# Value products of the recurrent mixer ahead of the weight group in the odd steps

## The chip, the cores and the metric

The kernel runs on one core of one Trainium2 chip. The metric is the device time of one execution in microseconds (us). Before the change it is 2569.6 us, the median of 3 runs (2569.27 to 2570.37).

## The reference

A sequence of 512 tokens of width 1024 goes through one first block and then two hybrid layers. A hybrid layer normalizes its input, projects it with a wide matrix, and gives the result to four mixers: a recurrent one (A, an mLSTM in both directions), grouped-query attention (B), neighbourhood attention (C) and differential attention (D). Each mixer's output is projected up, gated and added; an output projection and a feed-forward network follow. The change touches mixer A alone:

```
h_fwd = mlstm_scan(qh, kh, vh, i_fwd, jax.nn.log_sigmoid(f_fwd))
flip = lambda t: jnp.flip(t, axis=2)
h_bwd = flip(mlstm_scan(flip(qh), flip(kh), flip(vh), flip(i_bwd), flip(jax.nn.log_sigmoid(f_bwd))))
h = h_fwd + h_bwd
```

with 4 heads of width 128. The kernel computes it without the recurrence, as two masked products: for each head and direction P = (k q) x exp(decay mask), then the numerator P v and the denominator P 1, and the quotient with max(|denominator|, exp(-m)).

## The kernel before, in words

All tokens stand on chip in 4 tiles of 128. Each dense projection is a *block*: its weights come in units of 2 x 128 rows and 512 columns (512 KB), through 3 raw slots and 2 split slots. SyncE's queue loads a unit when the raw slot is free (L527), ScalarE makes its high part wH (L1046), VectorE the low part wL (L1591), and TensorE multiplies high by high, low by high and high by low. The function `group` (L638, L641) does this for one unit and one output tile: 2 row chunks x 3 = 6 matmuls of 512 columns. A group counts `groups` up, which lets ScalarE reuse a split slot.

The mixer is the function `mlstm`, with 36 steps, in each of the two layers; the profile shows them from about 444.6 and 1558.8 us. Its side work is a list of 36 groups (the blocks G00, G01 and the first unit of CQ), one for each step, which keep TensorE supplied while ScalarE and VectorE work on the scan. Steps 0 to 31 go through head h = s // 8, key chunk j = (s % 8) // 2, and direction: an even step is forward, an odd one (back = 1) backward. One step on TensorE, in the old order:

1. the mask product into bank 6 (TP): a row product (L824), 128 to 512 columns wide, and a bf16 causal mask (L826); it waits for the exponential of the step before (e_done);
2. even steps only: the scores k q into bank 4 or 5 (L834), used by this step and the next;
3. the weight group of the side work (L641);
4. the value product (L852), t + 1 chunks forward or 4 - t backward, each chunk two matmuls of 129 columns in the trace, into the one bank 7 (PV).

ScalarE takes the exponential of the mask (L1470). VectorE multiplies it with the scores into pmat (L2385, counts p_done), and drains the value product with four instructions that depend on each other: L2395, L2396, L2398 and L2404 (forward, writes) or L2401 (backward, adds); the last counts hh_done. Then every fourth step (s % 4 == 1) VectorE splits a weight unit (L1591).

Which value product a step carries is written in SCAN_VALUES. An odd step s < 32 has the forward product of its own head and tile. An even step from 8 on has a backward product of the head before. Steps 32 to 35 have the last head's backward products, in banks 7 and 6 in turn. A value product waits for

```python
pe.wait_ge(S["p_done"], i0 + (8 * (h + 1) if back else s))
if s == 1:
    evacuated(by_name[(l + 1, "AV")])
...
if nth >= 1:
    pe.wait_ge(S["hh_done"], nth - 1 if tail else nth)
```

that is, for the multiplications of all steps before it (forward), and for the drain of the value product before it (in the tail: the one before that). In step 1 it also waits until ScalarE has evacuated block AV, the values. The order on VectorE is: multiplication of step s, drain of the product of step s, split. On ScalarE: exponential of step s, then a split (s % 4 == 0) or a gate evacuation (L1145). The multiplication of an odd step stands behind the drain of the even step before it.

Of the kernel before, what the change touches and what calls it, by code (L numbers as in the profile page):

```python
# [271 lines left out]
def scan_step(s):  # L272

    h, j, back = s // 8, s % 8 // 2, s % 2
    lo, hi = (0, (j + 1) * P) if back else (j * P, SEQ)
    return h, j, back, lo, hi
# [23 lines left out]
def build(nc, a, out):  # L300
# [8 lines left out]
    with ctx:  # L309
# [156 lines left out]
        def wsrc(b, k0, kn):  # L466
            name, _, l = b.weight.partition(":")
            w = a[name]
            w = w[int(l) if l else 0]
            return w[b.row0 + k0 * P:b.row0 + (k0 + kn) * P, b.col0:b.col0 + b.cols].rearrange(  # L470
                "(k p) n -> p k n", p=P)
# [5 lines left out]
        def w_views(u):  # L477
            b, k0, kn, _ = units[u]
            width = P if b.gates else b.cols
            return [w[:, u % W_SLOTS, 0:kn * width].rearrange("p (k n) -> p k n", k=kn) for w in (wH, wL)]  # L480
# [65 lines left out]
        def _(pool):  # L546
# [23 lines left out]
            for g, (_, (ki, half)) in list(enumerate(row_groups(fox_items())))[2:]:  # L570
                r = slice(DH * half, DH * half + DH)
                pool.wait_ge(S["hi_done"], g + 1)
                pool.tensor_tensor(k_low[g % 2][r, :], k2[r, ki, :], k_twice[g % 2][r, :].bitcast(F32),
                                   ALU.subtract).then_inc(S["k_low_done"], 1)
# [39 lines left out]
        def _(pe):  # L614
# [3 lines left out]
            def group(b, i, t, chunk=None):  # L618

                u = b.first_unit + i  # L620
                _, k0, kn, _ = units[u]
                if t == 0:
                    pe.wait_ge(S["w_lo"], u + 1)
                if i == 0 and b.nth[b.bank0 + t]:
                    pe.wait_ge(free[b.bank0 + t], b.nth[b.bank0 + t])
                H, L = (hH, hL) if b.src == "h" else (yH, yL)
                vh, vl = w_views(u)
                for kk in range(kn):
                    k = k0 + kk
                    for j in (0, 1, 2) if chunk is None else (0, 2, 1):  # L630
                        if chunk is not None and j < 2:
                            pe.wait_ge(S["tp_free" if j else "tp_hi"], chunk[j] + kk + 1)
                        act_part = (H, L, H)[j]
                        w_part = (vh, vh, vl)[j]
                        first = i == 0 and kk == 0 and j == 0
                        last = i == len(b.units) - 1 and kk == kn - 1 and j == 2
                        if b.orient == "tok":
                            mm = pe.matmul(bank[t][:, 0:b.cols], act_part[:, k, t * P:(t + 1) * P], w_part[:, kk, :],  # L638
                                           start=first, stop=last)
                        else:  # L640
                            mm = pe.matmul(bank[b.bank0 + t][:, :], w_part[:, kk, t * P:(t + 1) * P], act_part[:, k, :],  # L641
                                           start=first, stop=last)
                mm.then_inc(S["groups"], 1)
# [165 lines left out]
            def evacuated(b):  # L809

                for j in range(b.banks):
                    pe.wait_ge(free[j], b.nth[j] + 1)

            def mlstm(l, side):


                i0 = 32 * l
                for s in range(36):
                    if s < 32:
                        i, (h, j, back, lo, hi) = i0 + s, scan_step(s)  # L820
                        row = 32 * back + h
                        if i >= 1:
                            pe.wait_ge(S["e_done"], i)
                        pe.matmul(bank[TP][:, lo:hi], row_sel[0:SPLIT_ROWS, row:row + 1].to_broadcast([SPLIT_ROWS, P]),  # L824
                                  row_nm[0:SPLIT_ROWS, lo:hi], start=True, stop=True)
                        pe.matmul(bank[TP][:, j * P:(j + 1) * P], ident16[:, :], (causal16 if back else anti16)[:, :],  # L826
                                  start=False, stop=True, skip_group_check=True).then_inc(S["mb_done"], 1)
                        if not back:
                            pair = i // 2
                            if pair >= 2:  # L830
                                pe.wait_ge(S["p_done"], 2 * (pair - 1))
                            if j == 0:
                                pe.wait_ge(S["qk_ready"], 9 * l + 6 + h)
                            pe.matmul(bank[SC + pair % 2][:, :], k1[:, h, j * P:(j + 1) * P], q1[:, h, :],  # L834
                                      start=True, stop=True).then_inc(S["qk_done"], 1)
                    if s < len(side):
                        group(*side[s])
                    if s in SCAN_VALUES:
                        h, t, back = SCAN_VALUES[s]
                        nth = i0 + SCAN_ORDER.index((h, t, back))  # L840
# [3 lines that stand above are left out]
                        tail = s > 32  # L844
                        if tail:
                            pe.wait_ge(S["e_done"], i0 + 32)
                        if nth >= 1:
                            pe.wait_ge(S["hh_done"], nth - 1 if tail else nth)
                        dst = bank[PV - (s % 2 if tail else 0)]
                        srcs = range(t, NT) if back else range(t + 1)  # L850
                        for sj in srcs:
                            mm = pe.matmul(dst[:, 0:P + 1], pmat[:, back, sj, t * P:(t + 1) * P],  # L852
                                           v1a[:, sj, h, :], start=sj == srcs[0], stop=sj == srcs[-1])
                        mm.then_inc(S["o_done"], 1)

            def hgrn_keys():

                pe.wait_ge(S["ke_ready"], 1)
                for m in range(3):
                    for g in range(2):  # L860
                        mm = pe.transpose(bank[TP + m // 2][:, (2 * (m % 2) + g) * P:(2 * (m % 2) + g + 1) * P],
                                          ke[:, g, m * P:(m + 1) * P], ident[:, :])
                    mm.then_inc(S["keT_done"], 1)
# [81 lines left out]
            for l in range(DEPTH):  # L945
# [25 lines left out]
                dense(L, "AV", between=b_transposes)  # L971
                pe.wait_ge(S["tp_free"], n.at("tp"))
                mlstm(l, side_groups(B("G00", "G01"), B("CQ")[0]))
                dense(L, "CQ", start=1)
                dense(L, "AO")
# [45 lines left out]
        def _(act):  # L1021
# [131 lines left out]
            def split_rows(items, g, q, k, blocks=(), after=None):  # L1153


                for b in blocks:
                    for t in range(b.banks):
                        act.wait_ge(free[t], b.nth[t] + 1)
                (qi, half), (ki, _) = row_groups(items)[g]
                r = slice(DH * half, DH * half + DH)  # L1160
                if g < 2:
                    act.wait_ge(S["groups"], after.groups_end)
                else:
                    act.wait_ge(S["sc_done"], n.at("items") - len(items) + NT * (g - 1))
                ins = A(q_split[g % 2][r, :], q[r, qi, :], ACT.Copy,
                        scale=1.0 if items[0]["kind"] in ("nat", "diff") else SCALE)
                if not keeps_k(items, g):
                    A(k_twice[g % 2][0:DH, :], k[r, ki, :], ACT.Copy)
                    if items[0]["kind"] == "fox" and g >= 2:
                        return  # L1170
                    ins = A(k_twice[g % 2][DH:P, :], k[r, ki, :], ACT.Copy)
                ins.then_inc(S["hi_done"], 1)
# [1444 lines left out]
```

## Time and profile before

| | |
|---|---|
| median of 3 runs | 2569.6 us |
| the profiled execution | 2569.09 us |
| its span in the profile | 2567.3 us |
| TensorE busy | 2535.3 us, 99% |
| VectorE busy | 1472.8 us, 57% |
| ScalarE busy | 1098.1 us, 43% |
| granted TensorE clock, mean | 0.997 |

The page gives each engine's busy time as a share of the span, and the chain of work that ended last, followed back from the end. PE is TensorE's matmuls, PEld its weight loads, DVE is VectorE, ACT ScalarE. A timeline row gives the start in us, the duration in us, the engine, the line, the operation with what it writes and reads, and in brackets the idle time before it and what ended it. Matmuls are pipelined: a 512-column matmul lasts 0.39 us, but the next starts after 0.23.

### The profile page before, as it was taken

The page shows a single profiled execution, that of the slowest core. Times are in us where ns is not written, and L with a number is a line of the kernel's source. Part 1 is how long each engine was busy: PE and PEld are TensorE (multiplying, and loading weights), DVE is VectorE, ACT ScalarE, POOL GpSimd, SP SyncE. Part 2 cuts the span into 40 slices and gives each one's busy share as a digit, 9 for nine tenths or more (in the row PEclk, how much of TensorE's full clock was granted, in tenths as well). Part 3 has the DMA queues.
Part 4 walks back from the last instruction along what each step waited for, and adds up shares of the span by engine and source line. Part 5 has one row for each costly group of instructions (what it writes and reads, how often), then busy time and mean ns, then how long its engine had stood idle before and what let it go on. Part 6 is the DMA issues. An engine that isn't in the chain of part 4 may idle for free.

```text
span 2567.3 us, 33046 instructions
## 1 busy us (share of the span) xinstructions
PE 2535.3 (99%) x12706; PEld 2110.5 (82%) x12706; DVE 1472.8 (57%) x2780; ACT 1098.1 (43%) x1929; POOL 45.1 (2%) x76
## 2 busy tenths in 40 slices
PE   8999999999999999999999999999999999999998
PEld 7888878788888888888888787888888887888887
DVE  6766668653536678644444686644447586544445
ACT  3436455333644566332222444335536483422223
POOL 0001000000000000000000000000000000000000
PEclk9999999999999999999999999999999999999999
DMA  4320223123313321233333232233132322333332
GB/s 148 90 67 30 79 59 103 50 82 99 91 59 96 82 86 57 70 112 98 99 99 96 78 95 62 66 99 113 44 92 69 97 72 80 93 99 99 96 94 90
DMA packets 118172, 217.54 MB, mean 85 GB/s; under 512 B 14080, under 2 KB 21552, under 8 KB 118016
## 3 DMA queue, kind: packets, MB, share of 16 engines
q1 hardware_dynamic: 114096, 201.60, 26.3%
q0 software_dynamic: 3776, 13.57, 2.0%
q8 instruction: 102, 1.67, 0.3%
q14 instruction: 54, 0.44, 0.1%
q10 hardware_dynamic: 144, 0.26, 0.0%
HBM read 211.20 MB, written 4.19 MB: 84 GB/s over the span
## 4 chain that ended last, share of the span: by engine, by line
PE 93%; DVE 4%; ACT 2%; issue 1%; DMA 0%; SPq 0%; ACTq 0%; DVEq 0%
PE bank L641 52%; PE bank L638 25%; PE bank L797 5%; PE bank L786 2%; PE bank L766 2%; PE bank L767 2%; PE bank L852 1%; PE bank L834 1%; PE bank L889 1%; PE bank L684 1%; DVE wL L1591 0%; DVE hL L1698 0%; PE bank L824 0%; PE bank L698 0%; DMA wraw<-in_w_in_dram 0%
## 5 line engine op out<-in xcount | busy, mean ns | idle before, releaser
L1591 DVE TENSOR_TENSOR wL<-wraw,wH 128x1024 fp32r<-128x1024 f32 (+1 forms) x388 | 460.3, 1186 | 646.0 <-ACT wH L1046 643.6
L1046 ACT ACTIVATE wH<-wraw 128x1024 fp32r<-128x1024 f32 (+1 forms) x388 | 398.2, 1026 | 888.0 <-PE bank L641 538.4
L641 PE MATMUL bank<-hH,wH 128*128 128x512 f32 x1720 | 691.6, 402 | 1.7 <-ACT hH L1123 0.9
L641 PE MATMUL bank<-hL,wH 128*128 128x512 f32 x1720 | 672.8, 391 | 0.0
L641 PE MATMUL bank<-hH,wL 128*128 128x512 f32 x1720 | 672.2, 391 | 0.0
L641 PEld LDWEIGHTS bank<-hH,wH 128*128 128x128 f32 x1720 | 324.0, 188 | 75.1 <-issue 8.9
L641 PEld LDWEIGHTS bank<-hL,wH 128*128 128x128 f32 x1720 | 323.8, 188 | 71.3 <-issue 7.6
L641 PEld LDWEIGHTS bank<-hH,wL 128*128 128x128 f32 x1720 | 323.4, 188 | 69.0
L638 PE MATMUL bank<-wH,hH 128*128 128x512 f32 (+1 forms) x736 | 283.1, 385 | 0.7 <-DVE wL L1591 0.7
L638 PE MATMUL bank<-wH,hL 128*128 128x512 f32 (+1 forms) x736 | 277.9, 378 | 0.0
L638 PE MATMUL bank<-wL,hH 128*128 128x512 f32 (+1 forms) x736 | 277.8, 377 | 0.0
L638 PEld LDWEIGHTS bank<-wH,hH 128*128 128x128 f32 x736 | 139.6, 190 | 26.7 <-DVE wL L1591 1.6
L797 PE MATMUL bank<-set,sbufPT 128*128 128x64 f32 (+1 forms) x1184 | 157.3, 270 | 3.8 <-DVE ytok L1806 2.3
L638 PEld LDWEIGHTS bank<-wL,hH 128*128 128x128 f32 x736 | 139.3, 189 | 25.8
L638 PEld LDWEIGHTS bank<-wH,hL 128*128 128x128 f32 x736 | 139.3, 189 | 23.9
L797 PEld LDWEIGHTS bank<-set,sbufPT 128*128 128x128 f32 x1184 | 147.4, 192 | 9.1 <-issue 7.2
L638 PE MATMUL bank<-wH,yH 128*128 128x512 f32 x352 | 137.4, 390 | 1.0 <-DVE yL L2519 1.0
L638 PE MATMUL bank<-wH,yL 128*128 128x512 f32 x352 | 137.1, 389 | 0.0
L638 PE MATMUL bank<-wL,yH 128*128 128x512 f32 x352 | 137.0, 389 | 0.0
L1211 ACT ACTIVATE sbufPT<-bank 128x512 f32<-128x512 f32 (+2 forms) x192 | 94.5, 492 | 38.9 <-PE bank L786 38.0
L1799 DVE RECIPROCAL small<-small 128x1 f32<-128x1 f32 x192 | 31.1, 162 | 131.1 <-PE bank L797 129.6
L641 PE MATMUL bank<-yH,wH 128*128 128x512 f32 x256 | 100.5, 392 | 0.9 <-ACT yH L1123 0.5
(338 smaller groups left out, 3135.4 us busy)
## 6 DMA issues: line engine op xcount, KB each, us to landing
wraw<-in_w_in_dram SPq DMA_DIRECT2D x180, 512.0 KB, 3.6
wraw<-in_w_ffn_down_dram SPq DMA_DIRECT2D x44, 512.0 KB, 3.6
wraw<-in_w_ffn_gate_dram SPq DMA_DIRECT2D x40, 512.0 KB, 3.6
wraw<-in_w_ffn_up_dram SPq DMA_DIRECT2D x40, 512.0 KB, 3.6
wraw<-in_w_out_dram SPq DMA_DIRECT2D x24, 512.0 KB, 3.6
wraw<-in_w_up_a_dram SPq DMA_DIRECT2D x8, 512.0 KB, 3.6
wraw<-in_w_up_b_dram SPq DMA_DIRECT2D x8, 512.0 KB, 3.7
wraw<-in_w_up_c_dram SPq DMA_DIRECT2D x8, 512.0 KB, 3.6
```

The lines of the kernel that those rows point to most:

```text
L638: mm = pe.matmul(bank[t][:, 0:b.cols], act_part[:, k, t * P:(t + 1) * P], w_part[:, kk, :], start=first, stop=last)
L641: mm = pe.matmul(bank[b.bank0 + t][:, :], w_part[:, kk, t * P:(t + 1) * P], act_part[:, k, :], start=first, stop=last)
L684: mm = pe.transpose(dst[:, t * P:(t + 1) * P], src[:, t, k * P:(k + 1) * P], ident[:, :])
L766: pe.matmul(dst[:, 0:kmax], q_split[slot][:, tok], k_twice[slot][:, keys], start=True, stop=False)
L767: mm = pe.matmul(dst[:, 0:kmax], q_split[slot][:, tok], k_low[slot][:, keys], start=False, stop=kind != "fox")
L786: mm = pe.transpose(bank[TP][:, c * P:(c + 1) * P], sbufS[:, y % 3, c * P:(c + 1) * P], ident[:, :])
L797: mm = pe.matmul(bank[PV][:, 0:w], sbufPT[:, y % 2, c * P:(c + 1) * P], (nat_values(it["t"], c) if kind == "nat" else v[:, c, :])[:, c0:c0 ...
L834: pe.matmul(bank[SC + pair % 2][:, :], k1[:, h, j * P:(j + 1) * P], q1[:, h, :], start=True, stop=True).then_inc(S["qk_done"], 1)
L1046: A(wH[:, u % W_SLOTS, 0:width], wraw[:, u % RAW_SLOTS, 0:width], ACT.Copy).then_inc(S["w_hi"], 1)
L1211: A(sbufPT[:, y % 2, 0:it["kmax"]], bank[TP][:, 0:it["kmax"]], ACT.Copy).then_inc(S["ptev"], 1)
L1591: V.tensor_tensor(wL[:, u % W_SLOTS, 0:width], wraw[:, u % RAW_SLOTS, 0:width], wH[:, u % W_SLOTS, 0:width].bitcast(F32), ALU.subtract).th ...
L1799: then(V.reciprocal(r, total))
```

## The change

In the odd steps the weight group is issued behind the value product, in both layers. In the even steps everything stays.

```diff
@@ -833,7 +833,7 @@
                             pe.matmul(bank[SC + pair % 2][:, :], k1[:, h, j * P:(j + 1) * P], q1[:, h, :],
                                       start=True, stop=True).then_inc(S["qk_done"], 1)
-                    if s < len(side):
+                    if s < len(side) and s % 2 == 0:
                         group(*side[s])
                     if s in SCAN_VALUES:
                         h, t, back = SCAN_VALUES[s]
@@ -852,6 +852,8 @@
                             mm = pe.matmul(dst[:, 0:P + 1], pmat[:, back, sj, t * P:(t + 1) * P],
                                            v1a[:, sj, h, :], start=sj == srcs[0], stop=sj == srcs[-1])
                         mm.then_inc(S["o_done"], 1)
+                    if s < len(side) and s % 2:
+                        group(*side[s])
```

## Rows read from the trace of the kernel before

**Rows 1.** The page: busy time by engine, and the chain that ended last.

```profile
PE 2535.3 (99%) x12706; PEld 2110.5 (82%) x12706; DVE 1472.8 (57%) x2780; ACT 1098.1 (43%) x1929; POOL 45.1 (2%) x76
PE 93%; DVE 4%; ACT 2%; issue 1%; DMA 0%; SPq 0%; ACTq 0%; DVEq 0%
```

**Rows 2.** Windows: length, busy us of PE, PEld, DVE, ACT, POOL, granted clock, DMA.

```profile
444.60:528.90 84.30, 84.30 (x440) 65.46 (x439) 50.42 (x154) 31.33 (x52) 0.00 (x0) 1.00 0.20 57
1003.00:1015.00 12.00, 9.97 (x64) 7.71 (x63) 8.76 (x28) 8.75 (x24) 0.00 (x0) 1.00 0.00 1
```

**Rows 3.** Chain through the second mixer; waits of 440 to 520 (total, times, longest).

```profile
by line: PE bank L641 55.2%; PE bank L852 19.0%; PE bank L834 16.8%; PE bank L824 5.3%; PE bank L826 2.7%; PE bank L638 1.3%
...
DVE small L2395 <- PE bank L852: 20.0, 25, 1.4
```

**Rows 4.** Timeline of steps 8 and 9 of the first mixer.

```profile
465.11 0.69 DVE L2385 SCALAR_TENSOR_TENSOR merged<-bank,sbufS 128x512 f32<-128x512 f32 x1 [0.38 <-PE bank L834]
466.13 1.06 PE L852 MATMUL bank<-set,merged 128*128 128x129 f32 x8
467.09 0.23 PE L826 MATMUL bank<-causal,ident 128*128 128x128 bf16 x1
467.13 0.48 PE L641 MATMUL bank<-hH,wH 128*128 128x512 f32 x1
467.23 0.16 DVE L2395 TENSOR_SCALAR small<-bank 128x1 f32<-128x1 f32 x1 [1.43 <-PE bank L852]
467.45 0.39 PE L641 MATMUL bank<-hL,wH 128*128 128x512 f32 x1
467.68 0.39 PE L641 MATMUL bank<-hH,wL 128*128 128x512 f32 x1
467.87 0.35 DVE L2401 SCALAR_TENSOR_TENSOR ytok<-bank,small,ytok 128x128 f32<-128x128 f32 x1
468.61 0.38 PE L852 MATMUL bank<-set,merged 128*128 128x129 f32 x2
```

**Rows 5.** Timeline of the difference heads: a value product that waits, one that doesn't.

```profile
1000.91 1.06 PE L797 MATMUL bank<-set,sbufPT 128*128 128x128 f32 x8
...
1005.39 0.35 DVE L1806 TENSOR_SCALAR ytok<-bank,small 128x128 f32<-128x128 f32 x1
...
1005.85 0.97 PEld L797 LDWEIGHTS bank<-set,sbufPT 128*128 128x128 f32 x8 [0.43 <-issue]
1005.88 1.13 PE L797 MATMUL bank<-set,sbufPT 128*128 128x128 f32 x8 [0.22 <-DVE ytok L1806]
```

**Rows 6.** Timeline, steps 10 to 15: backward products, the groups after them, VectorE in step 10.

```profile
470.06 1.22 DVE L1591 TENSOR_TENSOR wL<-wraw,wH 128x1024 fp32r<-128x1024 f32 x1
471.20 0.55 DVE L2385 SCALAR_TENSOR_TENSOR merged<-bank,sbufS 128x384 f32<-128x384 f32 x1
471.38 0.83 PE L852 MATMUL bank<-set,merged 128*128 128x129 f32 x6
472.21 0.48 PE L641 MATMUL bank<-hH,wH 128*128 128x512 f32 x1
476.60 0.60 PE L852 MATMUL bank<-set,merged 128*128 128x129 f32 x4
477.26 0.47 PE L641 MATMUL bank<-hH,wH 128*128 128x512 f32 x1
481.85 0.39 PE L852 MATMUL bank<-set,merged 128*128 128x129 f32 x2
482.34 0.48 PE L641 MATMUL bank<-hH,wH 128*128 128x512 f32 x1
```

**Rows 7.** Timeline of step 1, and the multiplication of step 2.

```profile
446.66 0.69 DVE L2385 SCALAR_TENSOR_TENSOR merged<-bank,sbufS 128x512 f32<-128x512 f32 x1 [1.41 <-ACT sbufS L1470]
447.30 0.47 PE L641 MATMUL bank<-hH,wH 128*128 128x512 f32 x1
451.35 0.55 DVE L2385 SCALAR_TENSOR_TENSOR merged<-bank,sbufS 128x384 f32<-128x384 f32 x1
```

## The prediction

> **What bounds the kernel now.** I read the page first: TensorE is busy 99% of the span and carries 93% of the chain that ended last [rows 1]. Then the table by windows: in the first layer's recurrent mixer (444.6 to 528.9 us) TensorE is busy for every microsecond at a granted clock of 1.00, while VectorE works 50 of 84 us and ScalarE 31 [rows 2]. The chain through the second layer's mixer names TensorE lines alone, and the waits of the stretch 440 to 520 us show VectorE's drain waiting for the value product (L852), 25 times, never the reverse [rows 3]. So in the mixers TensorE has no idle time to give away: a wait put into its stream is added to the span, unless TensorE waits later for something that this delay would have covered. Nothing of that sort shows; the whole of [rows 3] is other engines waiting for TensorE.
>
> **What the change moves.** Nothing is added or removed. In the odd steps (backward mask) the stream was: mask product, weight group of six matmuls, value product. Now it is: mask product, value product, group. An odd step's value product is a *forward* one; the *backward* value products sit at the end of the even steps from step 8 on, and stay there. So the order around an odd step s >= 9 becomes: backward value product (step s-1), mask product (s), forward value product (s), group (s). Both value products write the one bank PV, and the second waits (hh_done) until VectorE has drained the first. Before, mask product and group lay between them; now only the mask product does. No DMA moves, and the queues of SP and POOL are not passed: weight slots are released by the same groups in the same order.
>
> **The bank wait, step by step.** In [rows 4], steps 8 and 9: the backward product starts at 466.13 and its eight matmuls end at 467.19. VectorE begins to drain at 467.23 (L2395), and the last of its four instructions (L2401) ends at 467.87 + 0.35 = 468.22: 1.03 after the product's end. The group starts at 467.13, its second matmul 0.32 later and its third 0.23 after that, the usual spacing; so the group's real slot begins about 0.09 late, at 467.22. That is where the forward product would go if it had not to wait. Its other wait (p_done) is no matter: step 8's multiplication ended at 465.11 + 0.69 = 465.80.
>
> What restarting costs after such a wait is seen in the attention of the difference heads [rows 5]: VectorE's L1806 ends at 1005.39 + 0.35 = 1005.74, the waiting value product's weight load starts at 1005.85 and its first matmul at 1005.88, 0.14 after the drain; the eight then take 1.13, against 1.06 for eight that did not wait, 0.07 more. The stall is thus (1.03 + 0.14 + 0.07) from the end of the backward product, less the slot at G + 0.09, G being the start of the group in the old order. With the ends and starts of [rows 4, 6]:
> - step 9 (four chunks in step 8): 467.19 + 1.24 - 467.22 = 1.21
> - step 11 (three): 472.21 + 1.24 - 472.30 = 1.15
> - step 13 (two): 477.20 + 1.24 - 477.35 = 1.09
> - step 15 (one): 482.24 + 1.24 - 482.43 = 1.05
>
> It falls a little because the mask product of the odd step widens from 128 to 512 columns. Together 4.50 us for the eight steps of a head. Such pairs exist for heads 1, 2 and 3 (steps 9 to 31), in two layers: 6 x 4.50 = 27.0 us, 24 waits. Behind the waiting product stand, in order, its own group, the next mask product and the scores; ScalarE and VectorE wait for these and shift with them, and they were waiting for TensorE anyway.
>
> The Trainium skill ("TensorE: Matmul & The Clock Gate", Part 2) says that TensorE pulls weight loads ahead of matmuls in flight. If it did so past this wait, the 0.07 of the slow restart would vanish and the sum would be 25.3. In [rows 5] the load itself starts only 0.11 after the drain, so here it stood behind the wait; I keep 27.0.
>
> **The other odd steps.** Steps 1 to 7 have no backward value product before them; the forward one waits for VectorE's multiplication of the even step before (p_done). In step 1 that ends at 446.66 + 0.69 = 447.35 [rows 7]; plus 0.14 and 0.07 it is 447.56, against a slot at 447.30 + 0.09: 0.17 us, 0.3 over two layers. The values' own evacuation (AV) is by then over, since ScalarE did it before its first exponential of the mixer. In step 3 the multiplication ended late, at 451.90, because a weight split stood before it, just behind the drain; now product 1 comes a whole group earlier, so do its drain and the split, and the wait should be gone when step 3 asks. I put steps 3, 5, 7 at nothing: the cover is the even step's group, and if it were gone each would cost at most the 0.2 of step 1, under 1.5 us in all. In the tail, steps 33 and 35, the products use two banks in turn and ask only for the drain before last; one and two groups lie between. Nothing there.
>
> **The opposite direction.** Forward product (odd) to the next backward one (even): 468.61 to 471.38 before [rows 4, 6], which held a mask product, the scores and one group; now there is one group more, for a drain of 1.03. Nothing is waited for, and nothing was before, so this slack buys nothing.
>
> **A small term in between.** The 0.09 that a group loses behind the bf16 mask product may be lost no more, or may return behind the value product: 36 moved groups x 0.09 = 3.2 us, either way. In the 24 waits I have already taken it as saved; in the other 12 I put nothing.
>
> **Sum.** 27.0 + 0.3 = 27.3 us, on the profiled execution's 2569.1: 2596.4. That execution stands 0.5 under the median of 2569.6, so as a median: 2597.
>
> Bounds: the drain alone, with a restart at once and no slow first matmul, gives 24 x (1.12 - 0.21) = 22, less 1.1 for the 0.09 in the other 12 groups: 21, or 2590. On the upper side a whole weight load of 0.19 exposed at every restart, 4.6, and the 0.09 paid again by all 36: 27.3 + 4.6 + 3.2 = 35, or 2605.
>
> **Rivals.**
> - *No wait shows (within 0.2%).* If the drain were overlapped in some way, or the even step's mask product were longer than I think, up to 5 us would remain. Against it: the drain's four instructions depend on each other, all end 1.03 after the product, and the mask product takes 0.13 in [rows 4]. It gives 2570 to 2574. Chance 0.05.
> - *Faster.* The moved products lose the awkward place behind the group and the group the awkward place behind the bf16 product: -3.2 us from the 0.09 above, and the drain of every forward product starts 1.38 us earlier. It decides if the bank wait is below 0.13 per step, 24 x 0.13 = 3.2; then 2566. For it speaks only that first-matmul spacing; against it [rows 4]. Even whole it is within the noise. Chance 0.03, of which I give 0.02 to more than 0.2%.
> - *Slower by more.* VectorE comes late to the drain, because a multiplication or a weight split (1.22) is in its way. In step 10 the split of 470.06 pushes the multiplication to 471.20 to 471.75 [rows 6], only 0.46 before the backward product ends. But with the change drain and split come earlier against the backward product by a group. If it did happen, an odd step would wait for a multiplication of about 0.55 too: 24 x (1.12 + 0.55) = 40, 2610. A fall of the clock belongs here as well: a stretch in which TensorE was busy 9.97 of 12 us kept 1.00 [rows 2], and the mixers would be busier than about 80%, so I hardly count it. Chance 0.06.
>
> **How the numbers follow.** The forecast has 0.86. What a measurement of this kernel can tell is 0.2%, some 5 us; so faster 0.02, same 0.05, slower 0.93. The range 2589 to 2605 takes in both bounds of the forecast and leaves out the rivals, 0.14.
>
> **What would show it.** In the changed kernel's waits a new row: L852 waiting for VectorE's L2401, 24 times, with about 1.1 to 1.2 us each of idle TensorE; each mixer some 13.5 us longer (84.3 becomes 98), TensorE's busy time unchanged, clock 1.00, and nothing longer elsewhere. VectorE's drain after a backward product still 1.03 long. The forecast is wrong if L852 does not wait, if it waits for another line (a multiplication, an exponential), if steps 1 to 7 stall as well, or if stages outside the mixers take a part of the loss back.

## The result, and the profile after

The changed kernel takes 2597.8 us (median of 4 runs, 2595.96 to 2600.95), the kernel before 2569.7 (4 runs, 2569.27 to 2570.37). The ratio is 1.0108 with a 95% interval of 1.0096 to 1.0121: 28 us slower. The profiled execution took 2597.96 us, with a span of 2596.2.

Page of the kernel after: busy time by engine, and the chain that ended last, by engine.

```profile
PE 2540.1 (98%) x12706; PEld 2109.8 (81%) x12706; DVE 1474.4 (57%) x2780; ACT 1098.0 (42%) x1929; POOL 45.2 (2%) x76
PE 92%; DVE 5%; ACT 2%; issue 1%; DMA 0%; SPq 0%; ACTq 0%; DVEq 0%
```

Against [rows 1] the instruction counts are the same and the span is 28.9 us longer. The line numbers behind the edited place have moved by two: L2395 is now L2397, L2401 is L2403, L2385 is L2387.

Windows of the kernel after over the two mixers (columns as in [rows 2]).

```profile
445.60:543.80 98.20, 86.65 (x439) 65.31 (x438) 50.76 (x154) 31.04 (x52) 0.00 (x0) 1.00 0.16 49
1573.70:1671.80 98.10, 86.58 (x438) 65.25 (x437) 50.68 (x154) 30.93 (x52) 0.00 (x0) 1.00 0.16 49
```

A mixer took 84.3 us with TensorE never idle [rows 2]; now TensorE is idle for 98.20 - 86.65 = 11.55 us of it. The clock is still 1.00. What it waits for stands in the table of waits, restricted to TensorE (total, times, longest), of which these are the first four rows:

```profile
PE bank L852 <- DVE ytok L2403: 23.1, 24, 1.0
PE bank L698 <- DMA small<-in_norm_gT_dram: 7.9, 1, 7.9
PE bank L698 <- DVE merged L1659: 5.6, 6, 3.0
PE bank L797 <- DVE ytok L1808: 2.3, 6, 0.7
```

The first row is new: the value product waits for the last instruction of a backward drain, 24 times. In the kernel before, no row of this table names L852. Here is one of them, the timeline of steps 8 and 9 of the first mixer, to be laid beside [rows 4].

```profile
467.34 1.06 PE L852 MATMUL bank<-set,merged 128*128 128x129 f32 x8
468.15 0.31 PE L824 MATMUL bank<-row_nm,row_sel 100*128 100x128 f32 x1
468.30 0.23 PE L826 MATMUL bank<-causal,ident 128*128 128x128 bf16 x1
468.43 0.16 DVE L2397 TENSOR_SCALAR small<-bank 128x1 f32<-128x1 f32 x1 [1.43 <-PE bank L852]
...
469.08 0.35 DVE L2403 SCALAR_TENSOR_TENSOR ytok<-bank,small,ytok 128x128 f32<-128x128 f32 x1
...
469.54 0.30 PEld L852 LDWEIGHTS bank<-set,merged 128*128 128x128 f32 x2 [1.15 <-issue]
469.57 0.46 PE L852 MATMUL bank<-set,merged 128*128 128x129 f32 x2 [1.05 <-DVE ytok L2403]
469.79 0.48 PE L641 MATMUL bank<-hH,wH 128*128 128x512 f32 x1
470.10 0.39 PE L641 MATMUL bank<-hL,wH 128*128 128x512 f32 x1
...
471.27 0.34 PE L824 MATMUL bank<-row_nm,row_sel 100*128 100x384 f32 x1
...
474.40 0.36 PE L824 MATMUL bank<-row_nm,row_sel 100*128 100x256 f32 x1
```

The backward product ends at 467.34 + 1.06 = 468.40. The drain runs from 468.43 to 469.43, 1.03 after it. The weight load of the forward product starts at 469.54 and its first matmul at 469.57: 1.17 after the backward product's end, the 1.03 + 0.14 of the working above. The group, which used to fill this time, follows.

The length of a step is read from one mask product's start (L824) to the next. Before, they stood here (timeline of the kernel before, steps 9 to 12):

```profile
466.94 0.31 PE L824 MATMUL bank<-row_nm,row_sel 100*128 100x128 f32 x1
468.75 0.42 PE L824 MATMUL bank<-row_nm,row_sel 100*128 100x384 f32 x1
471.96 0.36 PE L824 MATMUL bank<-row_nm,row_sel 100*128 100x256 f32 x1
474.03 0.36 PE L824 MATMUL bank<-row_nm,row_sel 100*128 100x256 f32 x1
```

Step 9 was 1.81 us long and is 471.27 - 468.15 = 3.12; step 10 was 3.21 and is 3.13. Taken so over a head, the odd steps 9, 11, 13 and 15 grow by 1.31, 1.26, 1.20 and 1.16 us, 4.93 in all, and the even ones shrink by 0.08 each: 4.6 net. The other heads and the second mixer repeat these figures within 0.03.

Outside the mixers nothing gives anything back. From the mixer's first mask product (444.59 before, 445.63 after) to the first transposition of its result (view of L684, the load's first start) it was 144.4 us and is 158.4:

```profile
L684 PEld LDWEIGHTS bank<-ident,ytok x16: 138/141/142, 589.0 to 590.8; 128*128 128x128 f32 x16
```

```profile
L684 PEld LDWEIGHTS bank<-ident,ytok x16: 138/141/142, 604.0 to 605.8; 128*128 128x128 f32 x16
```

The first row is of before, the second of after. That is 14.0 us in this layer. The second mixer begins with these mask products, before and after:

```profile
1558.76 0.39 PE L824 MATMUL bank<-row_nm,row_sel 100*128 100x512 f32 x1
```

```profile
1573.67 0.39 PE L824 MATMUL bank<-row_nm,row_sel 100*128 100x512 f32 x1
```

From there to the end of the span it was 2567.3 - 1558.76 = 1008.5 us and is 2596.2 - 1573.67 = 1022.5, again 14.0 more. That makes 28 of the span's 28.9; the remaining 1.0 was there before the first mixer began and varies from run to run: in the runs below that point lies between 444.3 and 448.3 us, with nothing changed ahead of it.

### The profile page after: what moved, and what is told of

Its sections match the earlier page's. It is cut to its first block, busy times and chain, and to the rows that moved or that the text cites. A ratio compares the mean times of both kernels' runs of the same rounds, so it can differ in the third digit from the quotient of the medians.

```text
span 2596.2 us, 33046 instructions
## 1 busy us (share of the span) xinstructions
PE 2540.1 (98%) x12706; PEld 2109.8 (81%) x12706; DVE 1474.4 (57%) x2780; ACT 1098.0 (42%) x1929; POOL 45.2 (2%) x76
## 4 chain that ended last, share of the span: by engine, by line
PE 92%; DVE 5%; ACT 2%; issue 1%; DMA 0%; SPq 0%; ACTq 0%; DVEq 0%
PE bank L641 51%; PE bank L638 25%; PE bank L797 5%; PE bank L786 2%; PE bank L766 2%; PE bank L852 2%; PE bank L767 2%; PE bank L834 1%; PE bank L891 1%; PE bank L684 1%; DVE wL L1593 0%; DVE hL L1700 0%; DMA wraw<-in_w_in_dram 0%; DVE ytok L2403 0%; PE bank L698 0%
```

## The experiments

**E1, the group behind the value product in every step.** The odd steps have the changed order, but a group lies between any two value products again. Against the changed kernel the edit is:

```diff
-                    if s < len(side) and s % 2 == 0:
-                        group(*side[s])
                     if s in SCAN_VALUES:
...
-                    if s < len(side) and s % 2:
+                    if s < len(side):
                         group(*side[s])
```

> In every step, even ones too, the group stands behind the value product. Theory (the wait is the drain of the one bank: only the time between two value products counts): between the backward and the forward product lie a group and a mask product again, 1.38 + 0.13 us against the 1.24 that drain and restart take, so the 24 waits go, and the time is 2570 to 2573 us. Rival (a value product directly behind the mask product is itself dear, by the change of matmul kind or because VectorE hasn't finished its multiplication): the even steps now pay as well, 2598 us or more.

Measured 2571.5 us (10 runs), ratio to before 1.0007 (0.9997 to 1.0016). Timeline of steps 8 and 9 (L850 is the value product here):

```profile
468.76 0.94 PE L850 MATMUL bank<-set,merged 128*128 128x129 f32 x7
...
470.39 0.35 DVE L2401 SCALAR_TENSOR_TENSOR ytok<-bank,small,ytok 128x128 f32<-128x128 f32 x1
470.47 0.40 PE L641 MATMUL bank<-hL,wH 128*128 128x512 f32 x1
470.70 0.40 PE L641 MATMUL bank<-hH,wL 128*128 128x512 f32 x1
470.94 0.22 PE L824 MATMUL bank<-row_nm,row_sel 100*128 100x128 f32 x1
471.00 0.23 PE L826 MATMUL bank<-causal,ident 128*128 128x128 bf16 x1
471.07 0.44 PE L850 MATMUL bank<-set,merged 128*128 128x129 f32 x2
471.27 0.48 PE L641 MATMUL bank<-hH,wH 128*128 128x512 f32 x1
```

The odd step is in the same order as in the changed kernel: mask product, value product, group. But the drain ends at 470.74, and the forward product is due only at 471.07, with no wait. So it is not the place behind the mask product that costs; it is that the group has gone from between two products in one bank.

E1 has one wait of its own in each mixer, in step 32, which has no mask product:

```profile
528.79 1.13 PE L850 MATMUL bank<-set,merged 128*128 128x129 f32 x8
...
529.95 0.69 DVE L2385 SCALAR_TENSOR_TENSOR merged<-bank,sbufS 128x512 f32<-128x512 f32 x1 [1.31 <-PE bank L850]
...
530.56 0.15 DVE L2395 TENSOR_SCALAR small<-bank 128x1 f32<-128x1 f32 x1
...
531.20 0.35 DVE L2404 TENSOR_SCALAR ytok<-bank,small 128x128 f32<-128x128 f32 x1
...
531.69 1.13 PE L850 MATMUL bank<-set,merged 128*128 128x129 f32 x8 [0.38 <-DVE ytok L2404]
```

Here VectorE does a multiplication first and begins the drain 0.64 after the product's end (529.92) instead of 0.03. The drain then ends 1.63 after the product, and a whole group between the two products doesn't cover it: TensorE waits 0.38.

**E2, the changed order with two banks for the value products.**

```diff
-                            if pair >= 2:
-                                pe.wait_ge(S["p_done"], 2 * (pair - 1))
+                            if pair >= 1:
+                                pe.wait_ge(S["p_done"], 2 * pair)
-                            pe.matmul(bank[SC + pair % 2][:, :], k1[...], q1[...],
+                            pe.matmul(bank[SC][:, :], k1[...], q1[...],
-                        if nth >= 1:
-                            pe.wait_ge(S["hh_done"], nth - 1 if tail else nth)
-                        dst = bank[PV - (s % 2 if tail else 0)]
+                        if nth >= 2:
+                            pe.wait_ge(S["hh_done"], nth - 1)
+                        dst = bank[SC + 1 if nth % 2 else PV]
```

VectorE reads from the same banks.

> The changed order, but the value products use banks 7 and 5 in turn and wait for the drain before last; the scores have only bank 4 and wait for the multiplications of the pair before. Theory: no TensorE wait for VectorE's L2403 is left, and the odd steps are as long as before the change: 2570 to 2572 us. Rival (the order costs time by itself, or VectorE is too late for everything): 2590 us or more, with the wait on another line (p_done, L2387).

Measured 2569.5 us (10 runs), ratio 1.0002 (0.9993 to 1.0012). Timeline of steps 8 and 9:

```profile
465.14 0.31 PE L824 MATMUL bank<-row_nm,row_sel 100*128 100x128 f32 x1
465.35 0.44 PE L852 MATMUL bank<-set,merged 128*128 128x129 f32 x2
465.42 0.16 DVE L2397 TENSOR_SCALAR small<-bank 128x1 f32<-128x1 f32 x1 [1.43 <-PE bank L852]
465.55 0.48 PE L641 MATMUL bank<-hH,wH 128*128 128x512 f32 x1
...
466.06 0.35 DVE L2403 SCALAR_TENSOR_TENSOR ytok<-bank,small,ytok 128x128 f32<-128x128 f32 x1
...
467.02 0.33 PE L824 MATMUL bank<-row_nm,row_sel 100*128 100x384 f32 x1
...
470.16 0.36 PE L824 MATMUL bank<-row_nm,row_sel 100*128 100x256 f32 x1
```

The forward product starts at 465.35, before VectorE has begun to drain the backward one (465.42). The order is exactly the changed one and the whole loss is gone, so the loss was the single bank's. The rows of L824 show what the order does without a wait: step 9 takes 467.02 - 465.14 = 1.88 us, 0.07 more than before the change, and step 10 takes 3.14, 0.07 less. Of the 1.31 us by which step 9 grew in the changed kernel, 1.24 are the wait.

**E7, the same two banks in the old order**, the control for E2.

> The old order with the two banks of the experiment before: the control for it. Theory: the old order had no bank wait, so the second bank brings nothing, 2569 to 2570 us. Rival (the old order also lost something on the one bank, which the second one wins back): 2566 us or less.

Measured 2568.8 us (10 runs), ratio 0.9996 (0.9987 to 1.0006). No difference from before. The second bank has no worth of its own, and E2 is not a gain that hides a loss.

**E3, the value product of an odd step in the middle of its group.** `group` takes a function and calls it between its two row chunks, after three of its six matmuls; the code of the value product has become the function `product`. The even steps have the old order.

```diff
                 for kk in range(kn):
+                    if kk and between:
+                        between()
...
+                    if s in SCAN_VALUES and s % 2 and s < 32:
+                        group(*side[s], between=product)
```

> In the odd steps the value product stands in the middle of the group, three matmuls before it and three behind. Theory: the three matmuls cover 0.69 of each wait of 1.16 us, 24 x 0.47 = 11 us are left: about 2581 us. Rival (the wait is all or nothing, or the break in the group costs time of its own): 2570 or 2598 us.

Measured 2580.2 us (5 runs), ratio 1.0044 (1.0029 to 1.0059), 11.1 us over before. The wait's row in the timeline of steps 8 and 9:

```profile
470.18 0.35 DVE L2407 SCALAR_TENSOR_TENSOR ytok<-bank,small,ytok 128x128 f32<-128x128 f32 x1
...
470.68 0.46 PE L852 MATMUL bank<-set,merged 128*128 128x129 f32 x2 [0.30 <-DVE ytok L2407]
```

The forward product still starts 0.15 behind the drain's end, and its table of waits lists 18 such waits of at most 0.3 us; the other six (steps 15, 23 and 31 of each mixer, the shortest ones) show up on the weight load alone, which lists 24. So the three matmuls have taken their share out of each wait. The cost is not all or nothing: 0.69 us of cover took off 17 of the 28 us, and 24 x 0.69 is 17.

**E4, a shorter drain.** In steps 8 to 32 (the condition takes in step 32 as well, where two groups lie before the next product in that bank) the drain of the backward products leaves out the three instructions for the denominator's reciprocal; the quotient is taken with an older value. Against the changed kernel:

```diff
-                        then(V.tensor_scalar(hden[:, 0:1], den, -1.0, None, ALU.mult))
...
+                        if not back or s > 32:
+                            then(V.tensor_scalar(hden[:, 0:1], den, -1.0, None, ALU.mult))
...
```

> The changed order; the drain of the backward products in steps 8 to 30 leaves out its first three instructions (the denominator's reciprocal) and scales by an old value, so it is one instruction. Theory: the drain ends 0.39 instead of 1.03 us after the product, each wait is 0.64 shorter: 24 x 0.64 = 15 us less than with the change, about 2582 us. Rival (the wait ends with something else on VectorE or ScalarE): less than 4 us gained, 2594 us or more.

Measured 2582.4 us (4 runs), ratio 1.0048 (1.0034 to 1.0063): 15.5 us under the changed kernel. Its steps 8 and 9:

```profile
466.37 1.06 PE L852 MATMUL bank<-set,merged 128*128 128x129 f32 x8
...
467.47 0.35 DVE L2404 SCALAR_TENSOR_TENSOR ytok<-bank,small,ytok 128x128 f32<-128x128 f32 x1 [1.43 <-PE bank L852]
...
467.96 0.46 PE L852 MATMUL bank<-set,merged 128*128 128x129 f32 x2 [0.40 <-DVE ytok L2404]
```

The one instruction ends 0.39 after the product, and the forward product starts 0.14 later. A drain that is 0.64 shorter makes each wait 0.64 shorter (24 x 0.64 = 15.4), so the drain's last instruction is what ends the wait.

**E5, the changed order in four steps of each mixer** (9, 11, 13, 15), and **E6, in the steps without a bank wait** (1, 3, 5, 7, 33, 35). E5 moves the group behind the value product in the steps given by this condition; in the others it stays ahead of it:

```diff
-                    if s < len(side) and s % 2:
+                    if s < len(side) and s % 2 and 8 < s < 16:
                         group(*side[s])
```

In E6 the condition is `not 8 < s < 32`.

> The changed order only in steps 9, 11, 13 and 15 of each mixer, 8 waits instead of 24. Theory (the cost is a sum of waits of single steps, none given back later): a third of the change's cost in these steps, 2 x 4.6 = 9.3 us: about 2578.5 us. Rival (the waits overlap with each other or are given back behind the mixer): clearly less than a third, under 2574 us.

> The changed order only in steps 1, 3, 5, 7, 33 and 35, where no backward product in the same bank stands just before. Theory: these cost 0.2 us a mixer, the wait of step 1 for the multiplication of step 0: 2569.6 us, not to be told from before. Rival (every odd step pays for standing behind the mask product): 12 x 0.5 us or more, 2575 us.

E5 measured 2578.5 us (5 runs), ratio 1.0036 (1.0021 to 1.0050), 9.1 us over before; E6 2569.3 us (10 runs), ratio 1.0002 (0.9993 to 1.0012). The wait of E5 in its table of waits:

```profile
PE bank L852 <- DVE ytok L2403: 7.7, 8, 1.0
```

Eight waits cost a third of what 24 do (7.7 of 23.1 us idle; 9.1 of 28 us), and nothing is made up later. The time of E6 can't be told from that of the old order.

## Why the prediction was right

**The bank wait.** Forecast: 24 waits of about 1.1 to 1.2 us, 27.0 us in all. There are 24, on the line named, each with the 1.03 to 1.04 of drain and the 0.14 to 0.15 of restart that were read from [rows 4, 5]. E1 and E2 remove the wait in two ways and leave the moved order alone; E3 and E4 change its two terms, cover and drain, by known amounts and get the forecast change of time. This cause is shown.

**The other odd steps.** Step 1 was put at 0.17 us; it is 0.2 longer (in the first mixer 1.92 instead of 1.70 from mask product to mask product). The restart in it isn't the one of [rows 5], though:

```profile
447.69 0.69 DVE L2387 SCALAR_TENSOR_TENSOR merged<-bank,sbufS 128x512 f32<-128x512 f32 x1 [1.41 <-ACT sbufS L1472]
...
448.44 0.49 PE L852 MATMUL bank<-set,merged 128*128 128x129 f32 x2
```

The multiplication ends at 448.38 and the value product starts 0.06 later, not 0.14. Steps 3, 5, 7 and the tail were put at nothing, and E6 finds nothing. In steps 3 to 7 the odd step is 0.07 to 0.11 us longer and the next even step 0.07 to 0.09 shorter, as in E2.

**The small term.** Here the working was wrong in its parts. I took the 0.09 that a group loses behind the bf16 product as saved in the 24 steps. It isn't: behind the value product the group's second matmul comes 470.10 - 469.79 = 0.31 after its first, as before. So the odd steps grow by 4.93 us a head and not 4.50. On the other side the even steps, whose own mask product now follows a group and no longer a value product, are 0.08 shorter, which I had not seen. The two almost cancel: 4.6 against 4.50 a head, 28 us against 27.3.

**The mask product.** The 0.13 us that the working gives for it (under the rivals, and again in the expectation of E1) is only the stretch from the start of its bf16 half, 467.09 in [rows 4], to the group's slot at 467.22. The row product (L824) starts before that, at 466.94, and both lie almost wholly ahead of the modelled end of the backward product: from that end, 467.19, to the slot it is 0.03. The sum used ends and slots and is not touched. But between the end of one product and the start of the next E1 has 471.07 - 469.70 = 1.37 us, and not 1.38 + 0.13.

**TensorE's busy time.** I said that it would be unchanged, with 1.1 to 1.2 us idle in each wait. It rose by 4.8 us, from 2535.3 to 2540.1, with the same instructions, and the idle time is 0.87 to 1.05 a wait. The records of matmuls overlap in a full pipeline: in [rows 4] the group starts 0.04 behind the start of the bf16 product, which lasts 0.23. Before a wait that last record stands alone (468.30 to 468.53). So the idle 23.1 us of the table of waits is less than the loss; the rest of each wait looks like work, and 23.1 + 4.8 = 27.9 makes up the loss of 28.

**The rivals.** "No wait shows" and "faster" fell with the 24 waits. "Slower by more" supposed that VectorE would come late to the drain; in all 24 waits it began 0.03 to 0.04 after the product's end (468.43 in the rows above), and the clock stayed at 1.00. What such a delay would cost is seen in step 32 of E1. The rule of the Trainium skill ("TensorE: Matmul & The Clock Gate", Part 2), that weight loads are pulled ahead, did not act past this wait: the load starts at 469.54, 0.11 behind the drain's end of 469.43, as in [rows 5]. Where there is no wait the trace agrees with it: the load for the group's matmul at 470.10 starts at 469.87, while the matmul of 469.79 is in flight.

**The place in the range.** The forecast of 2597 missed the median of 2597.8 by less than a microsecond, which is less than single executions of this kernel differ by (2595.96 to 2600.95). The waits were foreseen; that the forecast came this near is luck, as the two errors of opposite sign in the small term, +0.43 and -0.32 us a head, leave 0.7 us over six heads.

## What to carry to other kernels

Where one engine is never idle, the order of its work decides which delays of the others are hidden. Two uses of one buffer need between them as much other work as the drain and the restart take, here 1.24 us if the drain begins at once, and more if the draining engine has something else to do first. Look at both neighbours of a moved operation: the product came nearer to the one before it in the same bank, and that alone cost 28 us, while the same order is free with a second bank or with the even steps moved as well. Such a cost can be worked out before a run from a few rows: the end of the first use, the end of the drain, the slot that the second use would have had, and one wait of the same kind elsewhere in the trace.

## What was not expected of the hardware

A restart of TensorE behind the last instruction of a drain took the same wherever it was read: 0.11 to 0.12 us from the instruction's end to the weight load and 0.14 to 0.15 to the first matmul, in the attention heads, in the changed kernel, and in E3 and E4 too. It isn't the same for every wait: in step 1 of both mixers, in all kernels with the changed order there, the weight load and the first matmul start 0.05 to 0.06 after the end of the multiplication. Why the two differ is not shown. The start of a 512-column group is 0.09 us slow behind a bf16 mask product and behind a value product of 129 columns alike.
